# Low parts of the weights: which of them GpSimd makes and which VectorE, in a three-block transformer kernel

## The chip, the cores and the metric

The kernel runs on one core of one Trainium2 chip. The metric is the time of the device for one launch, in microseconds, median of three runs. The engines of the core are TensorE (PE in the profile, with its weight loads as PEld), VectorE (DVE), ScalarE (ACT), GpSimd (POOL) and SyncE (SP, which here only issues loads and stores).

## What is computed

256 tokens of width 1024 pass through a chain of residual parts, all in fp32:

```python
h = x
h = h + even_mixer(rmsnorm(h), ...)        # 1024 -> 2048, conv and pooling, -> 1024
h = h + conv_ffn(rmsnorm(h), ...)          # 1024 -> 2 x 2816, silu, -> 1024
h = h + odd_mixer(rmsnorm(h), ...)         # 16 heads of attention
h = h + conv_ffn(rmsnorm(h), ...)
h = rmsnorm(h)                             # end of the first block
h = h + attention_2(rmsnorm(h), ...)       # stick-breaking and differential heads
h = h + conv_ffn_2(rmsnorm(h), ...)        # gelu, both halves convolved
h = h + sigmoid(rmsnorm(h) @ w_ple_gate) * (p @ w_ple_proj)
return rmsnorm(h)
```

The products with weights are made in three passes. A weight w is rounded to its high part wh, the rest w - wh is its low part wl, the input is split in the same way, and TensorE adds wh·xh, wh·xl and wl·xh. So each weight tile costs one rounding (ScalarE), one subtraction (VectorE or GpSimd) and three matmuls.

## The kernel before, in words

**Tiling.** Channels lie on the 128 partitions, the 256 tokens along the free dimension. A *unit* is 128 output channels: 8 tiles of 128x128 weights (1024 columns), 11 in the down phases (1408 columns, half of the 22 input chunks), 10 in the last phase (1280 columns). Four units are a *quad*, and a ring of four slots `s` = 0 to 3 in `raw`, `wh` and `wl` holds one quad; as soon as TensorE is done with the unit in a slot, the unit one quad later can be made in its place.

**Phases** (`PHASES`, name and quads): even_in 4, even_out 2, up0 11, down0 4, qkv0 6, out0 2, up1 11, down1 4, qkv1 6, out1 2, up2 11, down2 4, ple 2. A phase works on its own results and at the same time makes the weights one quad ahead: in its last quad these are the weights of the first quad of the next phase (`ahead`). So the first quad of up1 is made in the last quad of out0, and so on. Three units of the second quad of out0 and out1 (`early_units`) are kept in free room of `ys` and are made already at the end of the attention.

**The steps of one unit.** SP loads `raw[s]` when the low part of the quad before is made (`lo_ready[s]`). ScalarE waits for the load and for TensorE to leave the slot, and rounds `wh` (line 480, `hi_ready`). Then `wl = raw - wh` is made by GpSimd (line 434) if the slot is in `POOL_SLOTS` of the phase, else by VectorE (line 785, called by `split_ahead`); both raise `lo_ready[s]`, on which TensorE waits (lines 1243 to 1245 are the three matmuls of a tile). In `POOL_SLOTS` slots 0 and 2 of every phase are GpSimd's, none in qkv0 and qkv1, all four in ple.

**The order** is written out by hand in each engine's program, one block for an engine, and semaphores join them; nothing is scheduled by a tool. What stands around the change:

- `residual_out` (even_out, out0, out1). For each of 8 chunks m of `h`: VectorE adds the result to `h` (line 928, `bank_read`), then makes a low part of the weights if the slot is its own, then the low part of the next layer's input `xs` (line 801), then adds the square into `acc` (line 809). ScalarE between them makes the high part of `xs` (line 502) and the square (497). The next phase's first two units wait on TensorE for the chunks of `xs` one after the other.
- `residual_down`: the same for two chunks in a quad (line 950 adds).
- `up`: per quad two pairs of gate and value; VectorE reads the bank (824), does the taps of the convolution (833), the product (975) and its low part (979), and its `split_ahead` stands before the read of the next bank.
- `attention`: at the end VectorE makes the low part of an output (828), for layer 1 scales `h` by the norm in the middle (line 1182), and goes on to `residual_out`, whose first step clears `acc` (918).
- ple: per chunk VectorE reads (824), `split_ahead`, adds the square of the chunk before (809), multiplies by the gate (1215) and adds to `h` (1218); ScalarE rounds the weights ahead (480), makes the sigmoid (768), waits for `h`, squares it (497) and scales it (774). After the last chunk come the statistics, the root, the last scaling and the stores.

Of the kernel before, what the change touches and what calls it, by code (L numbers as in the profile page):

```python
# [55 lines left out]
PHASES = [("even_in", 4, DC), ("even_out", 2, DC), ("up0", 11, DC), ("down0", 4, HALF),  # L56
          ("qkv0", 6, DC), ("out0", 2, DC), ("up1", 11, DC), ("down1", 4, HALF),
          ("qkv1", 6, DC), ("out1", 2, DC), ("up2", 11, DC), ("down2", 4, HALF),
          ("ple", 2, DC + PLE)]


POOL_SLOTS = {name: (0, 2) for name, _, _ in PHASES} | {"qkv0": (), "qkv1": (), "ple": (0, 1, 2, 3)}


VECTORS = [("mix0", DC), ("ffn0", DC), ("mix1", DC), ("ffn1", DC), ("attn2", DC), ("ffn2", DC),
# [10 lines left out]
def build_program(nc, streams, x_in, p_in, vectors_in, pool_in, gate_in, rel_in, onehot_in, count_in, out):  # L76
# [4 lines left out]
    base, total = {}, 0  # L81
# [28 lines left out]
    def ahead(name, i, s):  # L110

        if isinstance(i, int) and i == quads_of[name] - 1:
            return (follow[name][0], base[follow[name][0]]) if name in follow else (None, None)
        return name, i + (base[name] + 1)
# [6 lines left out]
    def is_early(name, i, s):  # L121

        return isinstance(i, int) and (base[name] + i + 1, s) in early_units

    def final_unit(name, i, s):

        return isinstance(i, int) and i == quads_of[name] - 1 and s == RING - 1
# [4 lines left out]
    with ExitStack() as ctx:  # L132
# [189 lines left out]
        def split_weights(q, s, width):  # L322

            if isinstance(q, int) and (q, s) in early_units:
                at = PAIRS * 2 * SEQ + s * 2 * DC * P
                return flat_ys[:, at:at + DC * P], flat_ys[:, at + DC * P:at + 2 * DC * P]
            return wh[:, s, 0:width], wl[:, s, 0:width]
# [94 lines left out]
        @block.gpsimd  # L422
        def _(pool):
            steps = Steps(pool, pool_step)

            def split_phase(name, first, end, slots=None):
                tiles = tiles_of[name]

                def split_quad(i):
                    q = i + base[name]  # L430
                    for s in slots or POOL_SLOTS[name]:
                        pool.wait_ge(hi_ready, q * RING + s + 1)
                        high, low = split_weights(q, s, tiles * P)
                        nc.gpsimd.tensor_tensor(low, raw[:, s, 0:tiles * P], high.bitcast(f32), ALU.subtract)\  # L434
                          .then_inc(lo_ready[s], 1)

                if name in ("out0", "out1"):
                    for i in range(first, end):
                        split_quad(i)
                else:  # L440
                    each_quad(pool, first, end, split_quad)

            def pick(out_ap, compare, fill, at, pattern, per_row):
                return nc.gpsimd.affine_select(out=out_ap, in_=out_ap, compare_op=compare, fill=fill, base=at, pattern=pattern,
                                               channel_multiplier=per_row)


            split_phase("even_in", 0, 1, slots=(2,))
            nc.gpsimd.memset(neg_ones[:, :], -1.0)
            nc.gpsimd.memset(not_past, 0.0)  # L450
            nc.gpsimd.memset(neg_tri[:, :], -1.0)
            nc.gpsimd.memset(ident[:, :], 0.0)
            steps(nc.gpsimd.memset(sel_raw, 0.0))
            split_phase("even_in", 1, 2)
            pick(ident[:, :], ALU.not_equal, 1.0, 0, [[-1, P]], 1)
            pick(neg_tri[:, :], ALU.is_ge, 0.0, 0, [[-1, P]], 1)
            pick(not_past, ALU.is_gt, NEG, 0, [[1, P]], -1)
            split_phase("even_in", 2, 3)
            steps(pick(sel_raw, ALU.not_equal, HD ** 0.5, 0, [[-1, HEADS], [0, P]], 1))
            split_phase("even_in", 3, 4)  # L460
            pick(sel_raw, ALU.not_equal, HD ** 0.5, -HD, [[-1, HEADS], [0, P]], 1).then_inc(masks_ready, 1)
            for name, quads, _ in PHASES[1:]:
                if POOL_SLOTS[name]:
                    split_phase(name, 0, quads)

            pool.wait_ge(gained, POOL_OUT)
            pool.wait_ge(last_scale, 1)
            for m in range(POOL_OUT):
                nc.gpsimd.tensor_tensor(h[:, m, :], h[:, m, :], rstd[:, :], ALU.mult).then_inc(pool_out_ready, 1)
# [308 lines left out]
        def _(dve):  # L778
            steps = Steps(dve, dve_step)

            def split_unit(q, s, tiles):

                dve.wait_ge(hi_ready, q * RING + s + 1)
                high, low = split_weights(q, s, tiles * P)
                nc.vector.tensor_tensor(low, raw[:, s, 0:tiles * P], high.bitcast(f32), ALU.subtract).then_inc(lo_ready[s], 1)  # L785

            def split_ahead(name, i, s):

                target, q = ahead(name, i, s)
                if target and s not in POOL_SLOTS[target]:  # L790
                    split_unit(q, s, tiles_of[target])

            def phase(name, body, per_quad=0):
# [412 lines left out]
            for i in range(quads_of["ple"]):  # L1206
                q = i + base["ple"]
# [458 lines left out]
```

## Time and profile before

| | before |
|---|---|
| median of three runs | 968.26 us (967.33 to 969.67) |
| the profiled execution | 968.35 us, its span 966.6 us |
| PE busy | 934.3 us, 97% |
| PEld busy | 910.7 us, 94% |
| DVE busy | 649.6 us, 67% |
| ACT busy | 526.6 us, 54% |
| POOL busy | 314.7 us, 33% |
| mean granted clock of TensorE | 0.987 of full speed |

The profile is of one execution. Its times are counted from the first instruction; 1.75 us of the 968.35 lie outside the span. A timeline row gives start, duration, engine, line, operation, and in brackets the idle time of the engine before it with what ended it. Two instructions of one engine can overlap by some 0.1 us, since the record of one ends after the next has begun.

### The profile page before, as it was taken

To read this page: it belongs to the slowest core of one execution; us is meant where nothing else is said; L and a number is where in the kernel's file an instruction comes from. 1 tells how busy PE (TensorE), PEld (TensorE's weight loads), DVE (VectorE), ACT (ScalarE), POOL (GpSimd) and SP (SyncE) were. 2 spreads that over 40 slices of the span, in tenths; PEclk is the share of its full clock that TensorE was granted. 3 is DMA by queue.
4 is the path that set the end of the run, shared out by engine and by line. 5 is a ranking of instruction groups with operands and counts; after the bars stand their busy time and mean duration, and the time that the engine had idled before them with its cause. 6 is when DMAs were issued, how large, how long until landed. Compare 5 with 4: busy or idle time off the path is not lost.

```text
span 966.6 us, 20895 instructions
## 1 busy us (share of the span) xinstructions
PE 934.3 (97%) x7618; PEld 910.7 (94%) x7618; DVE 649.6 (67%) x1133; ACT 526.6 (54%) x847; POOL 314.7 (33%) x134
## 2 busy tenths in 40 slices
PE   8899999999998999999999999999999999999993
PEld 7789999999997999999999999989999999999993
DVE  6998676665456776676666555797557877765376
ACT  6345665555444555575555544556557766654443
POOL 3343343444410001334443441000224434444552
PEclk9899999999999999999999999999999999999997
DMA  7535865567542533375556754344335655665421
GB/s 245 184 110 196 229 221 192 183 201 251 183 146 87 171 135 119 123 234 186 186 175 195 233 182 135 125 155 141 107 106 180 194 187 185 188 218 192 159 81 45
DMA packets 46329, 163.52 MB, mean 169 GB/s; under 512 B 5010, under 2 KB 9746, under 8 KB 46277
## 3 DMA queue, kind: packets, MB, share of 16 engines
q1 hardware_dynamic: 41704, 158.19, 49.6%
q10 hardware_dynamic: 4573, 4.62, 1.8%
q8 instruction: 34, 0.56, 0.2%
q14 instruction: 18, 0.15, 0.0%
HBM read 161.71 MB, written 3.44 MB: 171 GB/s over the span
## 4 chain that ended last, share of the span: by engine, by line
PE 80%; DVE 8%; issue 6%; ACT 3%; POOL 1%; DMA 1%; SPq 0%; DVEq 0%; POOLq 0%; ACTq 0%
PE psum L1243 25%; PE psum L1244 24%; PE psum L1245 24%; POOL wl L434 1%; DVE h L1218 1%; PE psum L1415 1%; DMA raw<-in_even_in 1%; DVE wl L785 1%; ACT wh L480 1%; DVE work L882 1%; PE psum L1392 1%; DVE xs L801 1%; PE psum L1384 1%; PE psum L1356 1%; ACT xs L502 0%
## 5 line engine op out<-in xcount | busy, mean ns | idle before, releaser
L434 POOL TENSOR_TENSOR wl<-raw,wh 128x1024 fp32r<-128x1024 f32 (+2 forms) x113 | 297.3, 2631 | 614.9 <-ACT wh L480 614.8
L1243 PE MATMUL psum<-xs,wh 128*128 128x256 f32 x1632 | 467.8, 287 | 6.9 <-DVE wl L785 4.2
L1244 PE MATMUL psum<-xs,wh 128*128 128x256 f32 x1632 | 462.9, 284 | 0.0
L1245 PE MATMUL psum<-xs,wl 128*128 128x256 f32 x1632 | 462.8, 284 | 0.0
L480 ACT ACTIVATE wh<-raw 128x1024 fp32r<-128x1024 f32 (+2 forms) x270 | 301.2, 1119 | 264.6 <-PE psum L1245 252.8
L1243 PEld LDWEIGHTS psum<-xs,wh 128*128 128x128 f32 x1632 | 314.4, 193 | 13.7 <-DVE wl L785 5.4
L1244 PEld LDWEIGHTS psum<-xs,wh 128*128 128x128 f32 x1632 | 314.4, 193 | 0.2
L1245 PEld LDWEIGHTS psum<-xs,wl 128*128 128x128 f32 x1632 | 314.3, 193 | 0.0
L785 DVE TENSOR_TENSOR wl<-raw,wh 128x1024 fp32r<-128x1024 f32 (+1 forms) x157 | 203.9, 1301 | 99.4 <-ACT wh L480 99.0
L1243 PE MATMUL psum<-ys,wh 128*128 128x256 f32 x672 | 191.8, 285 | 0.0
L1244 PE MATMUL psum<-ys,wh 128*128 128x256 f32 x672 | 190.7, 284 | 0.0
L1245 PE MATMUL psum<-ys,wl 128*128 128x256 f32 x672 | 190.7, 284 | 0.0
L1243 PEld LDWEIGHTS psum<-ys,wh 128*128 128x128 f32 x672 | 129.6, 193 | 0.8 <-issue 0.7
L1244 PEld LDWEIGHTS psum<-ys,wh 128*128 128x128 f32 x672 | 129.6, 193 | 0.1
L1245 PEld LDWEIGHTS psum<-ys,wl 128*128 128x128 f32 x672 | 129.5, 193 | 0.0
L833 DVE SCALAR_TENSOR_TENSOR psum<-work,vec,psum 128x256 f32<-128x256 f32 x176 | 85.3, 485 | 56.1 <-ACT psum L591 53.0
L801 DVE SCALAR_TENSOR_TENSOR xs<-h,vec,xs 128x256 fp32r<-128x256 f32 (+1 forms) x56 | 61.0, 1098 | 29.1 <-ACT xs L502 28.7
L824 DVE TENSOR_TENSOR work<-psum,rstd 128x256 f32<-128x256 f32 x112 | 47.1, 421 | 19.8 <-PE psum L1245 19.1
L591 ACT ACTIVATE psum<-work,vec 128x256 f32<-128x256 f32 x88 | 49.4, 561 | 9.7 <-DVE work L824 9.4
L502 ACT ACTIVATE xs<-h,vec 128x256 fp32r<-128x256 f32 (+1 forms) x48 | 24.3, 506 | 40.4 <-DVE h L928 26.5
L641 ACT ACTIVATE work<-work,row_max 128x128 f32<-128x128 f32 (+1 forms) x48 | 21.3, 444 | 34.5 <-DVE row_max L1045 25.8
L1019 DVE TENSOR_TENSOR qkv<-psum,rstd 128x256 f32<-128x256 f32 x48 | 19.7, 418 | 15.7 <-PE psum L1245 15.7
(195 smaller groups left out, 708.6 us busy)
## 6 DMA issues: line engine op xcount, KB each, us to landing
raw<-in_up SPq DMA_DIRECT2D x132, 512.0 KB, 3.8
raw<-in_down SPq DMA_DIRECT2D x48, 704.0 KB, 4.3
raw<-in_qkv SPq DMA_DIRECT2D x48, 512.0 KB, 3.3
raw<-in_even_in SPq DMA_DIRECT2D x16, 512.0 KB, 4.2
raw<-in_out SPq DMA_DIRECT2D x16, 512.0 KB, 3.2
raw<-in_ple SPq DMA_DIRECT2D x8, 640.0 KB, 3.9
raw<-in_even_out SPq DMA_DIRECT2D x8, 512.0 KB, 3.3
toeplitz_dram<-table_dram ACTq DMA_DIRECT2D x1, 2048.0 KB
```

Of the source, the lines that this page charges most:

```text
L434: nc.gpsimd.tensor_tensor(low, raw[:, s, 0:tiles * P], high.bitcast(f32), ALU.subtract)\
L480: nc.scalar.activation(split_weights(q, s, tiles * P)[0], raw[:, s, 0:tiles * P], ACT.Copy).then_inc(hi_ready, 1)
L502: nc.scalar.activation(xs[:, ds(m, 1), 0, :], h[:, ds(m, 1), :], ACT.Identity, scale=column(VECTORS[n][0], m)).then_inc(xh_ready, 1)
L591: nc.scalar.activation(target, padded[:, 2:2 + SEQ], ACT.Identity, bias=column(bias_name, chunk), scale=column(taps, chunk + 2 * chunks)). ...
L641: last = nc.scalar.activation(e[:, half, a:z], e[:, half, a:z], ACT.Exp, bias=row_max[:, n % 2, at:at + 1], accum_out=row_sum[:, n % 2, at ...
L785: nc.vector.tensor_tensor(low, raw[:, s, 0:tiles * P], high.bitcast(f32), ALU.subtract).then_inc(lo_ready[s], 1)
L801: nc.vector.scalar_tensor_tensor(xs[:, ds(m, 1), 1, :], h[:, ds(m, 1), :], column(VECTORS[n][0], m), xs[:, ds(m, 1), 0, :].bitcast(f32), A ...
L824: return nc.vector.tensor_tensor(out_ap, proj[:, s, 0:SEQ], rstd[:, :], ALU.mult)
L833: return nc.vector.scalar_tensor_tensor(out_ap, padded[:, k:k + SEQ], column(taps, chunk + k * chunks), out_ap, ALU.mult, ALU.add)
L1243: nc.tensor.matmul(bank, high_w[:, w], high, start=first, stop=False)
L1244: nc.tensor.matmul(bank, high_w[:, w], low, start=False, stop=False)
L1245: done = nc.tensor.matmul(bank, low_w[:, w], high, start=False, stop=last)
```

## The change

`POOL_SLOTS` now has two entries for each phase: the slots that GpSimd makes in the first quad of the phase, and those in the others. A new helper `pool_slots(name, q)` picks the entry. GpSimd keeps slots 0 and 2 in the up phases behind their first quad, in even_in (slot 2 alone in the first quad), and in the first quad of even_out, out0 and out1. Everything else is VectorE's: the first quads of the up phases, the second quads of even_out, out0 and out1, the down phases and ple.

```diff
-POOL_SLOTS = {name: (0, 2) for name, _, _ in PHASES} | {"qkv0": (), "qkv1": (), "ple": (0, 1, 2, 3)}
+POOL_SLOTS = {name: ((), ()) for name, _, _ in PHASES}
+POOL_SLOTS |= {"even_in": ((2,), (0, 2)), "even_out": ((0, 2), ()), "out0": ((0, 2), ()), "out1": ((0, 2), ())}
+POOL_SLOTS |= {name: ((), (0, 2)) for name in ("up0", "up1", "up2")}
...
+    def pool_slots(name, q):
+
+        return POOL_SLOTS[name][0 if isinstance(q, int) and q == base[name] else 1]
...
-            def split_phase(name, first, end, slots=None):
+            def split_phase(name, first, end):
...
-                    for s in slots or POOL_SLOTS[name]:
+                    for s in pool_slots(name, q):
...
-                if POOL_SLOTS[name]:
-                    split_phase(name, 0, quads)
+
+                first, others = POOL_SLOTS[name]
+                if first:
+                    split_phase(name, 0, 1)
+                if others:
+                    split_phase(name, 1, quads)
...
-                if target and s not in POOL_SLOTS[target]:
+                if target and s not in pool_slots(target, q):
```

Counted over the program, GpSimd makes 117 low parts before and 73 after; 44 go to VectorE: 2 in even_out, 2 in the first quad of each up phase, 8 in each down phase, 2 in each of out0 and out1, and 8 in ple. No instruction of TensorE, ScalarE or SP is moved. Lines of the changed program are numbered 12 higher on VectorE (785 is 797, 1218 is 1230).

VectorE in ple, from the reciprocal of the norm on. Before:

```order
L819 RECIPROCAL rstd<-work 128x256
L918 MEMSET acc 128x256
L824 TENSOR_TENSOR work<-psum,rstd 128x256
L1215 TENSOR_TENSOR work<-psum,work 128x256
L1218 TENSOR_TENSOR h<-h,work 128x256
L824 TENSOR_TENSOR work<-psum,rstd 128x256
L809 TENSOR_TENSOR acc<-acc,work 128x256
L1215 TENSOR_TENSOR work<-psum,work 128x256
L1218 TENSOR_TENSOR h<-h,work 128x256
```

And after:

```order
L831 RECIPROCAL rstd<-work 128x256
L930 MEMSET acc 128x256
L836 TENSOR_TENSOR work<-psum,rstd 128x256
L797 TENSOR_TENSOR wl<-raw,wh 128x1280
L1227 TENSOR_TENSOR work<-psum,work 128x256
L1230 TENSOR_TENSOR h<-h,work 128x256
L836 TENSOR_TENSOR work<-psum,rstd 128x256
L797 TENSOR_TENSOR wl<-raw,wh 128x1280
L821 TENSOR_TENSOR acc<-acc,work 128x256
L1227 TENSOR_TENSOR work<-psum,work 128x256
L1230 TENSOR_TENSOR h<-h,work 128x256
```

In each of the first four chunks a low part of 1280 columns now stands between the read of the bank and the square.

VectorE at the end of the second attention (layer 1), going over into the residual of out1; `ys<-raw,ys` is the low part of an early unit. Before:

```order
L1092 SCALAR_TENSOR_TENSOR work<-work 128x768
L785 TENSOR_TENSOR ys<-raw,ys 128x1024
L1182 SCALAR_TENSOR_TENSOR h<-h,vec,mid_rstd 128x256
L828 TENSOR_TENSOR ys<-psum,ys 128x256
L1182 SCALAR_TENSOR_TENSOR h<-h,vec,mid_rstd 128x256
L918 MEMSET acc 128x256
L928 TENSOR_TENSOR h<-h,psum 128x256
```

And after:

```order
L1104 SCALAR_TENSOR_TENSOR work<-work 128x768
L797 TENSOR_TENSOR ys<-raw,ys 128x1024 x2
L1194 SCALAR_TENSOR_TENSOR h<-h,vec,mid_rstd 128x256
L840 TENSOR_TENSOR ys<-psum,ys 128x256
L797 TENSOR_TENSOR ys<-raw,ys 128x1024
L1194 SCALAR_TENSOR_TENSOR h<-h,vec,mid_rstd 128x256
L930 MEMSET acc 128x256
L940 TENSOR_TENSOR h<-h,psum 128x256
```

Two early low parts are new on this engine; the second of them stands right ahead of the first addition into `h`.

VectorE in the last quad of the residual of out1 (chunks 4 to 6), where the first quad of up2 is made. Before:

```order
L928 TENSOR_TENSOR h<-h,psum 128x256
L801 SCALAR_TENSOR_TENSOR xs<-h,vec,xs 128x256
L809 TENSOR_TENSOR acc<-acc,psum 128x256
L928 TENSOR_TENSOR h<-h,psum 128x256
L785 TENSOR_TENSOR wl<-raw,wh 128x1024
L801 SCALAR_TENSOR_TENSOR xs<-h,vec,xs 128x256
L809 TENSOR_TENSOR acc<-acc,psum 128x256
```

And after:

```order
L940 TENSOR_TENSOR h<-h,psum 128x256
L797 TENSOR_TENSOR wl<-raw,wh 128x1024
L813 SCALAR_TENSOR_TENSOR xs<-h,vec,xs 128x256
L821 TENSOR_TENSOR acc<-acc,psum 128x256
L940 TENSOR_TENSOR h<-h,psum 128x256
L797 TENSOR_TENSOR wl<-raw,wh 128x1024
L813 SCALAR_TENSOR_TENSOR xs<-h,vec,xs 128x256
L821 TENSOR_TENSOR acc<-acc,psum 128x256
```

Chunk 4 (and chunk 6 like it) now has a low part of 1024 columns on VectorE between its addition and its `xs`, as chunk 5 had before.

## Rows read from the trace of the kernel before

**Rows 1.** Busy time by stretch: us, PE, PEld, DVE, ACT, POOL (instructions), granted clock, DMA share, GB/s.

```profile
40.00:47.00 7.00, 7.00 (x26) 4.80 (x25) 5.85 (x11) 0.89 (x2) 0.00 (x0) 0.51 0.50 173
...
140.00:290.00 150.00, 150.00 (x1252) 150.00 (x1252) 87.37 (x142) 76.29 (x109) 57.23 (x21) 1.00 0.58 192
...
313.00:316.40 3.40, 3.40 (x18) 2.78 (x15) 3.37 (x7) 1.22 (x3) 0.00 (x0) 0.50 0.60 173
```

**Rows 2.** Waits of PE: line waited for, us in total, times, longest.

```profile
PE psum L1517 <- DVE work L891: 4.8, 2, 2.6
...
PE psum L1243 <- DVE xs L801: 2.5, 2, 1.3
PE psum L1392 <- DVE work L1065: 2.4, 1, 2.4
PE psum L1559 <- POOL wl L434: 1.2, 1, 1.2
```

**Rows 3.** Groups with shapes apart: busy us, mean ns | idle before.

```profile
L785 DVE TENSOR_TENSOR wl<-raw,wh 128x1024 fp32r<-128x1024 f32 x133 | 162.8, 1227 | 51.2 <-ACT wh L480 50.8
...
L785 DVE TENSOR_TENSOR wl<-raw,wh 128x1408 fp32r<-128x1408 f32 x24 | 41.1, 1712 | 48.2 <-ACT wh L480 48.2
...
L434 POOL TENSOR_TENSOR wl<-raw,wh 128x1280 fp32r<-128x1280 f32 x8 | 23.6, 2955 | 18.2 <-ACT wh L480 18.2
```

**Rows 4.** Timeline of DVE in the last quad of out0, chunks 4 to 6.

```profile
407.48 0.41 DVE L928 TENSOR_TENSOR h<-h,psum 128x256 f32<-128x256 f32 x1
...
410.51 0.41 DVE L928 TENSOR_TENSOR h<-h,psum 128x256 f32<-128x256 f32 x1
...
411.98 0.47 DVE L801 SCALAR_TENSOR_TENSOR xs<-h,vec,xs 128x256 fp32r<-128x256 f32 x1
...
412.71 0.41 DVE L928 TENSOR_TENSOR h<-h,psum 128x256 f32<-128x256 f32 x1
413.76 1.69 DVE L801 SCALAR_TENSOR_TENSOR xs<-h,vec,xs 128x256 fp32r<-128x256 f32 x1 [0.65 <-ACT xs L502]
```

**Rows 5.** Timeline of POOL and PE in the same stretch.

```profile
412.80 2.38 POOL L434 TENSOR_TENSOR wl<-raw,wh 128x1024 fp32r<-128x1024 f32 x1 [2.82 <-ACT wh L480]
...
415.51 0.38 PE L1243 MATMUL psum<-xs,wh 128*128 128x256 f32 x1 [1.35 <-DVE xs L801]
```

**Rows 6.** Timeline at the entry of out1's residual, DVE and PE.

```profile
714.40 0.42 DVE L828 TENSOR_TENSOR ys<-psum,ys 128x256 fp32r<-128x256 f32 x1 [1.60 <-ACT ys L544]
714.75 1.06 DVE L1182 SCALAR_TENSOR_TENSOR h<-h,vec,mid_rstd 128x256 f32<-128x256 f32 x1
...
716.23 0.42 DVE L928 TENSOR_TENSOR h<-h,psum 128x256 f32<-128x256 f32 x1
...
716.84 0.32 PE L1243 MATMUL psum<-ys 128*128 128x256 f32 x1
```

**Rows 7.** Timeline of DVE in ple: chunks 2, 3 and 7.

```profile
939.68 2.52 DVE L1218 TENSOR_TENSOR h<-h,work 128x256 f32<-128x256 f32 x1
...
944.56 0.42 DVE L1215 TENSOR_TENSOR work<-psum,work 128x256 f32<-128x256 f32 x1 [1.45 <-ACT work L768]
945.02 2.48 DVE L1218 TENSOR_TENSOR h<-h,work 128x256 f32<-128x256 f32 x1
...
955.36 0.42 DVE L1218 TENSOR_TENSOR h<-h,work 128x256 f32<-128x256 f32 x1
```

**Rows 8.** Timeline of ACT and PE in ple.

```profile
942.96 1.25 ACT L480 ACTIVATE wh<-raw 128x1280 fp32r<-128x1280 f32 x1
...
947.27 0.39 PE L1559 MATMUL psum<-ps,wh 128*128 128x256 f32 x1 [1.21 <-POOL wl L434]
```

**Rows 9.** Timeline: PE in up0's second quad; ACT and DVE at up2's end.

```profile
107.85 0.38 PE L1243 MATMUL psum<-xs,wh 128*128 128x256 f32 x1 [0.18 <-POOL wl L434]
...
857.18 1.38 ACT L480 ACTIVATE wh<-raw 128x1408 fp32r<-128x1408 f32 x1 [0.30 <-PE psum L1245]
...
857.74 0.41 DVE L824 TENSOR_TENSOR work<-psum,rstd 128x256 f32<-128x256 f32 x1
```

More of the change, by code:

```diff
@@ L445, in pick @@
                                                channel_multiplier=per_row)
-            split_phase("even_in", 0, 1, slots=(2,))
+            split_phase("even_in", 0, 1)
             nc.gpsimd.memset(neg_ones[:, :], -1.0)
```

## The prediction, made before the changed kernel was run

> **What bounds the kernel now.** I read the busy times by stretch first. In 140 to 290 us, which is up0 and down0, PE is busy all 150 us with 1252 matmuls, one every 0.12 us, at full clock, and DVE is busy 87 us and POOL 57 [rows 1]. The other up and down phases look the same. There TensorE alone sets the time, and work that goes from POOL to DVE is free as long as DVE keeps up. So only the places where PE waits can change. The list of PE's waits has them [rows 2]: 4.8 us on the pooling in even_in and 2.4 us in the first attention, neither near a moved instruction; 2.5 us on the `xs` chunks at out0 into up1 and out1 into up2; 1.2 us on a GpSimd low part in ple. Behind ple's last matmul the rest of the chain is DVE's and ACT's, so what DVE loses in ple is lost at the end.
>
> What the reader is to see in the timelines is how DVE and POOL hinder each other. The last `xs` low part before PE's wait (L801) took 1.69 us, the one before it, without POOL at work, 0.47 [rows 4]. It began at 413.76, behind a POOL low part that ran from 412.80 to 415.18, and it ended at 415.45, 0.27 us behind that [rows 5]. In ple L1218, two inputs from SBUF like L801, took 2.52 and 2.48 us beside POOL and 0.42 without [rows 7]. So a DVE instruction with two SBUF inputs that comes while POOL works waits until POOL is done. L928, which reads one input from PSUM, stays at 0.41 [rows 4].
>
> **The change part by part.** The sum is made against the profiled execution, 968.35 us with a span of 966.6; the median of the runs is 968.26, 0.1 below, which I leave out.
>
> Price of a moved low part on DVE: 1.22 us for 1024 columns [rows 3]. For 1408 columns the mean is 1.71 us, which holds some that waited for POOL [rows 3]; by the slope of 1024 columns a free one is 1.6. For 1280 columns, a size DVE never had, the two give 1.22 + 256 x 1.02 ns = 1.48. On POOL the same work is 2.96 [rows 3]. The 44 moved ones add some 62 us to DVE's 650, and nothing to PE.
>
> *Part 1, ple: on the path.* Take the end of L1218 as the beat. Before, it ends at 942.20 and 947.50, a beat of 5.3 us [rows 7]. In the beat ACT squares and scales, starts the rounding 0.76 us in and ends it at 2.01 [rows 8]; POOL starts on it, the gate follows, and L1218 waits for POOL. After, DVE makes the low part from 2.05 to 3.53, then the square (L809, 0.33 from start to start: L801 and L809 together take 0.73 from 411.98 to 412.71 [rows 4], 0.40 of it L801), then L1215 and L1218, 0.46 apart [rows 7], and 0.42 for the last: 3.45 + 0.34 + 0.46 + 0.42 = 4.67. The sigmoid is done by then. That is 0.65 a beat, and from chunk 0 to chunk 3 there are three: 1.95 us. Chunk 0 itself gains more: its L1218 loses its wait for POOL as well, some 1.9 us, against 1.48 for the low part, of which the wait for the gate hides about half a us; and in down2's last quad the `xs` low parts no longer wait for POOL, by which the norm's root comes some 0.6 us earlier. I take 1.65, from 0.6 to 1.8. The last four chunks go on at 2.07 a beat, (955.78 - 947.50) / 4 [rows 7], and the tail behind them doesn't change. PE isn't in the way: its last unit loses its wait of 1.21 and starts at 946.1 [rows 8], and with 30 matmuls of 0.12 it ends at 949.7, while the last L1218 would end at 955.8 - 3.6 = 952.2. **-3.6 us**, between -2.55 and -3.75.
>
> *Part 2, out0 into up1.* A step from addition to addition is 3.03 us with a POOL low part beside it (407.48 to 410.51) and 2.20 with a DVE one in it (410.51 to 412.71), since the DVE one lies in the 0.65 us in which DVE waits for ACT anyway [rows 4]. Chunks 4 and 6 change kind. Then chunk 6 is added at 407.48 + 2 x 2.20 = 411.88, and its `xs` is ready 1.94 us later (410.51 to 412.45 is the model), at 413.82, 1.63 us before the old 415.45. PE lost 1.35 by the record, 1.5 counted in its beat of 0.12 (the record of the last matmul lasts on), at 415.51 [rows 5]. Gain 1.5, with only 0.1 us of margin, so 0.8 to 1.5. Chunk 7 follows 1.8 later and is wanted 2.9 later. The early low part that is new ahead of out0's first addition is covered by DVE's wait for PE there. **-1.5 us**.
>
> *Part 3, out1 into up2.* The same two steps, but DVE has no pause at the entry. L828 at 714.40 is followed now by a low part of 1.22, then L1182, which loses its wait for POOL (1.06 becomes 0.47), then the addition: it moves from 716.23 to 716.23 + 1.13 - 0.59 = 716.77 [rows 6]. PE's first matmul of the second quad waits for that addition and started at 716.84, 0.2 us behind its end [rows 6]; now it starts at 717.3. Behind it are queued out1's whole second quad and up2. That is +0.45. Chunk 6 is ready 1.63 - 0.54 = 1.09 us earlier than before; PE, 0.45 late already, wants it 1.3 - 0.45 = 0.85 earlier: the wait, 2.5 - 1.35 = 1.15 by the record and 1.3 in PE's beat, is gone [rows 2, 5]. Bounds: +0.5 (the wait stays, too) to -1.3. **-0.85 us**.
>
> *Part 4, even_out into up0.* 0.18 us by the record, 0.3 in PE's beat, is lost at 107.85 on POOL's low part for up0's second quad [rows 9]. POOL still makes it, but the residual of even_out ends some 2 us earlier by the same steps, and ACT gets to that rounding earlier. **-0.3 us**, 0 to -0.3.
>
> *Part 5, down phases and the ends of the up phases: nothing.* A down quad lasts PE 132 x 0.12 = 15.8 us. DVE now has four low parts of 1.6 and two chunks of about 1.3 in it, 9 us; cover is 6 us, beyond which each us costs one, as it would in every quad. Its waits for ScalarE's rounding stand ahead of `xs`, which matters only in the last quad of down2, counted in part 1; down0 and down1 hand over to qkv, which VectorE made before, too. At the end of up2 two low parts of 1.6 come ahead of the read of the last bank, at 857.74 [rows 9]. PE had left the last unit of up2 by 857.18 and wants the bank 33 x 0.12 = 4.0 us later, at 861.1 [rows 9]. With the idle time that DVE had before its low parts I get the read's end at 860.0: 1.1 us of cover. up0 and up1, with fewer taps, have more.
>
> Sum: -3.6 - 1.5 - 0.85 - 0.3 = -6.25, so 968.35 - 6.25 = **962.1 us**. All parts at their bad ends give -2.55 - 0.8 + 0.5 = -2.85, 965.5; I set the end at 965.4, since not all four will fall there.
>
> *The clock.* After PE's waits of 2.6 and 2.4 us the granted clock went to 0.5, that is 1.2 GHz of 2.4, at 40 and at 313 us, for some 7 and 3.4 us [rows 1, 2]. Of the waits of up to 1.35 us none had such a stretch. In my forecast no new wait is over 0.5 us. A stretch of 3.4 us costs 1.7; the one at 313 us lies behind moved work and can go or double, which is +-1.7.
>
> The Trainium skill, TensorE: Matmul & The Clock Gate, Part 1, says that the window in which activity is judged runs freely, so that the same kernel can meet it at another phase. The two stretches of different length behind nearly equal waits agree with that. By it a shift alone could give 960.4 or 963.8 where the sum says 962.1.
>
> **Rivals.**
> - *Only ple gains.* The margin of part 2 is 0.1 us and part 3 has a loss of its own; if chunk 6 comes late in both, or waits turn up elsewhere, parts 2 to 4 are nothing: 968.35 - 3.6 = 964.7. For it: thin margins. Against: the 2.20 step is measured, not derived.
> - *A wash.* A POOL low part of 1024 columns holds up DVE for 1.2 us (1.69 less 0.47) and DVE's own takes 1.22 [rows 3, 4]: if the steps took as long with it, out0, out1 and ple would stay as they are, 968.3. Against: the step of 2.20, in which it hides behind ACT. In ple it can hide less, and there its 1.48 stands against 2.1 of waiting. The Trainium skill, Perfetto Trace Analysis, Optimizing Scalar/DVE Operations, says that the two engines share a read port, so that offloading between them might not help; read the other way round, it says that bringing work back might change nothing. The trace agrees on the sharing, and its steps of 3.03 and 2.20 speak against the second half. By that rule the time would be 968.3.
> - *Slower: DVE becomes the bound at the end of the up phases.* Without use of its idle time the two low parts put the last bank's read at 857.74 + 0.41 + 3.2 = 861.35, 0.25 us too late [rows 9]. The mechanism decides from 1.1 us more DVE work than I count; to make the kernel slower by 2 us it must eat the 6.25 as well, some 2.8 us at each of three places: 970.4. For it: this is where a moved low part stands ahead of a bank that PE needs. Against: nothing in the trace makes a DVE low part that slow but POOL, which is then silent.
> - *The change doesn't do what it says.* The order of instructions shows 44 moved; left out.
>
> **How the numbers follow.** The forecast, 960.4 to 964.4 with the clock's share, has 0.78; only ple, 964.7 (964.4 to 965.4), 0.10; the wash 0.07; slower 0.04; 0.01 is left for more gain than that. The range reaches from 960.0 to 965.4 and holds nearly 0.85. A measurement of this kernel can tell 0.2%, some 2 us, from no change; the cases give 0.88 faster, 0.08 within, 0.04 slower.
>
> **What would show it.** POOL busy falls from 315 to some 195 us, DVE's busy time rises by less than 62 us, since its waits behind POOL count as busy. L1218 is 0.42 in all eight chunks and the beat 4.7. PE's waits on L801 and on POOL in ple are gone; a new one of 0.4 to 0.5 us stands at the first matmul of out1's second quad. The low parts of 1408 columns on DVE have a mean of 1.6. I am wrong if PE waits in the down phases or at the banks of the last up quads, if the step of chunks 4 and 6 stays near 3.0, or if a new stretch at half clock follows one of these places.

## The result, and the profile after

The changed kernel takes 957.78 us (median of four runs, 956.27 to 959.12), the kernel before, in the same comparison, 967.83 (967.33 to 969.67): a ratio of 0.9903, 95% interval 0.9886 to 0.992. The forecast was 962.1, from 960.0 to 965.4. So the direction was right and the size was not: it is faster by 10 us here, and by some 8 us in the later comparisons (0.9916 and 0.9923). The forecast had 6.25. One run of the kernel before in a later comparison, 1002.13 us at a granted clock of 0.843, is a slow one and is left out of every mean below.

The profiled execution takes 957.83 us, with a span of 955.6. Busy times, after:

```profile
PE 930.6 (97%) x7618; PEld 908.9 (95%) x7618; DVE 663.7 (69%) x1177; ACT 525.6 (55%) x847; POOL 184.3 (19%) x90
```

GpSimd lost 130 us of work, and VectorE, which took it over, gained 14, where the forecast had put its new low parts at some 62. The groups with shapes apart (busy us, mean ns | idle before) say why; they answer [rows 3]:

```profile
L442 POOL TENSOR_TENSOR wl<-raw,wh 128x1024 fp32r<-128x1024 f32 x73 | 176.5, 2418 | 656.9 <-ACT wh L492 656.8
L797 DVE TENSOR_TENSOR wl<-raw,wh 128x1024 fp32r<-128x1024 f32 x141 | 172.9, 1229 | 53.7 <-ACT wh L492 53.5
L797 DVE TENSOR_TENSOR wl<-raw,wh 128x1408 fp32r<-128x1408 f32 x48 | 77.9, 1623 | 44.5 <-ACT wh L492 44.4
L813 DVE SCALAR_TENSOR_TENSOR xs<-h,vec,xs 128x256 fp32r<-128x256 f32 x38 | 17.8, 480 | 8.2 <-ACT xs L514 7.8 <-ACT xs L538 0.4
L797 DVE TENSOR_TENSOR wl<-raw,wh 128x1280 fp32r<-128x1280 f32 x8 | 11.9, 1493 | 10.5 <-ACT wh L492 10.5
```

The prices were right: 1408 columns take 1.62 us now (1.71 before, with waits behind GpSimd in it; forecast 1.6), 1280 take 1.49 (forecast 1.48). The `xs` low part, which had taken up to 2.93 us (a mean of 1.10), is 0.47 to 0.49 everywhere. What VectorE's record called busy had in part been waiting.

The waits of PE (line waited for, us in total, times, longest) answer [rows 2]:

```profile
PE psum L1529 <- DVE work L903: 4.8, 2, 2.6
...
PE psum L1404 <- DVE work L1077: 2.4, 1, 2.4
...
PE psum L1255 <- DVE h L940: 0.3, 1, 0.3
```

The waits on the `xs` chunks and the two on GpSimd's low parts are gone, and the new one at out1 is there. The waits left out of the list stand at the same places as before: at the start and in the mixer on VectorE's first low parts, in the attentions, and at the last statistics (2.2 us now, 4.4 before). Nothing has taken their place in the down phases.

**out0 into up1**, VectorE's timeline of chunks 5 to 7 after, answering [rows 4]:

```profile
404.65 0.41 DVE L940 TENSOR_TENSOR h<-h,psum 128x256 f32<-128x256 f32 x1
...
406.84 0.41 DVE L940 TENSOR_TENSOR h<-h,psum 128x256 f32<-128x256 f32 x1
407.17 1.21 DVE L797 TENSOR_TENSOR wl<-raw,wh 128x1024 fp32r<-128x1024 f32 x1
408.31 0.47 DVE L813 SCALAR_TENSOR_TENSOR xs<-h,vec,xs 128x256 fp32r<-128x256 f32 x1
...
409.04 0.41 DVE L940 TENSOR_TENSOR h<-h,psum 128x256 f32<-128x256 f32 x1
```

Every step (from addition to addition) is 2.20 us, where a step beside GpSimd had been 3.03.

**out1**, first step, DVE and PE, answering [rows 6]:

```profile
708.19 1.22 DVE L797 TENSOR_TENSOR ys<-raw,ys 128x1024 fp32r<-128x1024 f32 x1
709.32 0.48 DVE L1194 SCALAR_TENSOR_TENSOR h<-h,vec,mid_rstd 128x256 f32<-128x256 f32 x1
...
710.22 0.42 DVE L940 TENSOR_TENSOR h<-h,psum 128x256 f32<-128x256 f32 x1
...
710.79 0.35 PE L1255 MATMUL psum<-ys 128*128 128x256 f32 x1 [0.35 <-DVE h L940]
```

**ple**, DVE from chunk 1's addition to chunk 2's, and PE's first matmul behind the last chunk, answering [rows 7, 8]:

```profile
926.73 0.43 DVE L1230 TENSOR_TENSOR h<-h,work 128x256 f32<-128x256 f32 x1
...
929.20 1.49 DVE L797 TENSOR_TENSOR wl<-raw,wh 128x1280 fp32r<-128x1280 f32 x1 [1.71 <-ACT wh L492]
...
931.40 0.42 DVE L1230 TENSOR_TENSOR h<-h,work 128x256 f32<-128x256 f32 x1
...
944.48 0.74 PE L1581 MATMUL psum<-acc,ones 128*128 128x256 f32 x2 [2.22 <-DVE work L1227]
```

The beat is 4.67 us (926.73 to 931.40), as worked out, and the multiply-and-add into `h` is 0.42.

**The end of up2**, answering [rows 9]: the last bank's read stands at

```profile
852.15 0.42 DVE L836 TENSOR_TENSOR work<-psum,rstd 128x256 f32<-128x256 f32 x1
```

All of up2 lies 7.41 us earlier than before (the statistics matmul ahead of it, explained in the next section: 735.54 before, 728.13 after). Without the two low parts ahead of it the read would stand at 857.74 - 7.41 = 850.33, so they moved it by 1.82 us; the forecast had its end go from 858.15 to 860.0, 1.85. PE doesn't wait for it.

### The profile page after: what moved, and what is told of

The parts are those of the page before. It is cut to its first block, busy times and chain, and to the rows that moved or that the text cites. A ratio compares the mean times of both kernels' runs of the same rounds, so it can differ in the third digit from the quotient of the medians.

```text
span 955.6 us, 20828 instructions
## 1 busy us (share of the span) xinstructions
PE 930.6 (97%) x7618; PEld 908.9 (95%) x7618; DVE 663.7 (69%) x1177; ACT 525.6 (55%) x847; POOL 184.3 (19%) x90
## 4 chain that ended last, share of the span: by engine, by line
PE 88%; DVE 8%; ACT 2%; issue 1%; DMA 1%; SPq 0%; DVEq 0%; ACTq 0%
PE psum L1255 28%; PE psum L1256 27%; PE psum L1257 27%; DVE work L894 2%; DVE wl L797 1%; PE psum L1427 1%; DMA raw<-in_even_in 1%; PE psum L1404 1%; PE psum L1396 1%; ACT wh L492 1%; PE psum L1368 0%; PE psum L1366 0%; ACT work L653 0%; DVE work L836 0%; DVE acc L865 0%
## 5 line engine op out<-in xcount | busy, mean ns | idle before, releaser
L797 DVE TENSOR_TENSOR wl<-raw,wh 128x1024 fp32r<-128x1024 f32 (+2 forms) x197 | 262.8, 1336 | 108.8 <-ACT wh L492 108.4
L442 POOL TENSOR_TENSOR wl<-raw,wh 128x1024 fp32r<-128x1024 f32 x73 | 176.5, 2418 | 656.9 <-ACT wh L492 656.8
L813 DVE SCALAR_TENSOR_TENSOR xs<-h,vec,xs 128x256 fp32r<-128x256 f32 (+1 forms) x56 | 26.5, 480 | 8.2 <-ACT xs L514 7.8
```

Source lines behind the costliest of these rows:

```text
L813: nc.vector.scalar_tensor_tensor(xs[:, ds(m, 1), 1, :], h[:, ds(m, 1), :], column(VECTORS[n][0], m), xs[:, ds(m, 1), 0, :].bitcast(f32), A ...
```

## Where the time went, stretch by stretch

The sums of squares of the norms are made by a statistics matmul, which stands at a fixed place in PE's order; from one to the next PE has the same work in all kernels of this study. Four of their rows, before (a second execution of it) and after (a third):

```profile
290.84 0.60 PE L1274 MATMUL psum<-acc,ones 128*128 128x256 f32 x2
417.58 0.60 PE L1274 MATMUL psum<-acc,ones 128*128 128x256 f32 x2
```

```profile
288.98 0.60 PE L1286 MATMUL psum<-acc,ones 128*128 128x256 f32 x2
412.83 0.60 PE L1286 MATMUL psum<-acc,ones 128*128 128x256 f32 x2
```

Differences of such starts, us (each column one profiled execution; the variants are those of the experiments below):

| stretch | before | before, 2nd | after | after, 3rd | ple alone | up1's quad back |
|---|---|---|---|---|---|---|
| start to first statistics | 19.38 | 18.38 | 18.42 | 18.26 | 18.14 | 18.63 |
| to up0 (even mixer) | 81.95 | 81.18 | 79.65 | 79.83 | 81.17 | 81.11 |
| to qkv0 (up0, down0) | 191.12 | 191.28 | 190.71 | 190.89 | 190.50 | 190.50 |
| to up1 (attention, out0) | 126.74 | 126.74 | 123.86 | 123.85 | 125.28 | 125.28 |
| to qkv1 (up1, down1) | 190.50 | 190.50 | 190.49 | 190.50 | 190.50 | 190.50 |
| to up2 (attention, out1) | 125.85 | 125.87 | 125.00 | 125.02 | 125.87 | 124.99 |
| to ple (up2, down2) | 188.34 | 188.34 | 188.35 | 188.33 | 188.34 | 188.34 |
| to the last statistics | 31.60 | 31.58 | 28.00 | 27.99 | 28.00 | 27.99 |

The four places gave, between the recorded executions before and after, 3.60 in ple, 0.85 at out1, 0.41 in up0, and at out0 a part of 2.88. The rest of the 11.0 us of span is elsewhere: 0.96 at the start, where the first weights landed later in the first execution (its first weight matmul stood at 9.95 us, and at 8.1 to 9.3 in the others here), 2.30 in the even mixer, and the other part of the 2.88.

The 2.88 are 1.43 for the wait at out0 (put back in experiment 3) and 1.46 for a stretch at half clock that the first execution after doesn't have (priced in the section on the clock). Of the 2.30, one stretch of 3.4 us less is some 1.5. Most of the rest is a wait of 0.64 us on a low part of the weights that stands in this one trace alone:

```profile
28.13 0.39 PE L1243 MATMUL psum<-xs,wh 128*128 128x256 f32 x1 [0.64 <-DVE wl L785]
```

The second execution of the kernel before has the same stretches at half clock, not this wait, and 81.18 us there.

## The experiments

**1. The same two kernels again.**

> The kernel before, unchanged, to have its start and its stretches at half clock a second time. The places that the change touches account for 6.3 us of the 10; the other 4 lie ahead of or beside it: the first matmul on weights began 1.1 us earlier in the changed kernel's trace, 0.6 us more was gained by 28 us, and the trace has two stretches of half clock less (3 us). Theory A (chance of the execution): here the first matmul on weights starts anywhere from 8.8 to 10.0 us and the stretches at half clock differ in number or length from the first trace, while the waits behind moved work (1.35, 1.15 and 1.21 us) come back to within 0.1 us; ratio 1.000 to the kernel before, with single runs spread over 3 us. Theory B (something in the changed program brings it): start at 9.95 and stretches at 40, 70 and 313 us come back as they were.

> The changed kernel, unchanged. Theory A: over more runs the gain shrinks towards the 6.3 us of the named places, ratio 0.9925 to 0.9935, and single runs differ by 1.7 us steps with the mean granted clock (one stretch of 3.4 us each). Theory B: the gain stays at 10 us, ratio 0.989 to 0.991, start at 8.9 us.

> The kernel before once more, for its granted clock. Theory A1 (the short waits of 1.2 to 1.5 us at out0, out1 and in ple can be followed by half clock, depending on the execution): a stretch at half clock near 412, 730 or 945 us in one of the executions. A2 (only the long ones of 2.2 us and more): stretches only near 40, 70 and 310 us, as in both traces so far.

The kernel before again: 966.14 us (ratio 0.9987, 0.9973 to 1.0001); one more execution of it 967.84. The changed one: 958.32, ratio 0.9916, 0.9896 to 0.9936. All waits were there again with the same size (1.36, 1.16 and 1.19 us before; 0.35 after). So the waits belong to the kernels. The late start does not.

**2. One part alone.** Against the changed kernel's table, all phases as before but ple:

```diff
-POOL_SLOTS = {name: ((), ()) for name, _, _ in PHASES}
-POOL_SLOTS |= {"even_in": ((2,), (0, 2)), "even_out": ((0, 2), ()), "out0": ((0, 2), ()), "out1": ((0, 2), ())}
-POOL_SLOTS |= {name: ((), (0, 2)) for name in ("up0", "up1", "up2")}
+POOL_SLOTS = {name: ((0, 2), (0, 2)) for name, _, _ in PHASES}
+POOL_SLOTS |= {"even_in": ((2,), (0, 2)), "qkv0": ((), ()), "qkv1": ((), ()), "ple": ((0, 1, 2, 3), (0, 1, 2, 3))}
+POOL_SLOTS |= {"ple": ((), ())}
```

> Only ple's low parts go to VectorE, all else as before. From the places: -3.6 us, ratio 0.9963, L1218's twin at 0.42 in all chunks. Theory A: 0.9963 within 0.001. Theory B, if the extra comes with any change of the program's instructions: 0.992 to 0.993.

Measured: 962.56, ratio 0.9961 (0.9946 to 0.9976). In its trace the last stretch of the table is 28.00 against 31.6. Four of the others are those of before (81.17, 190.50 in up1, 125.87 and 188.34), and the waits at out0 and out1 are there; two are shorter without any moved work: 190.50 in up0, where PE has no wait on GpSimd's low part this time, and 125.28 at the attention, which here has no stretch at half clock:

```profile
309.00:313.00 4.00, 3.92 (x33) 3.42 (x34) 4.00 (x6) 2.58 (x4) 0.00 (x0) 1.00 0.32 93
```

Part 1 is worth 3.60 us and nothing of it depends on the other parts.

The same, with ple all GpSimd's as before, and the out phases and the up phases' first quads changed:

```diff
+POOL_SLOTS |= {name: ((0, 2), ()) for name in ("even_out", "out0", "out1")}
+POOL_SLOTS |= {name: ((), (0, 2)) for name in ("up0", "up1", "up2")}
```

> Only the second quads of even_out, out0, out1 and the first quads of the up phases go to VectorE. From the places: -0.3 -1.5 -0.85 = -2.65 us, ratio 0.9973; PE's waits on the xs chunks gone, one of 0.35 at out1's second quad. Theory A: 0.9973 within 0.001. Theory B: 0.993.

> The change at even_out, out0, out1 and the first quads of the up phases alone. Theory: apart from the clock it gives 2.9 us (its counted 2.65 and little more), and the rest that it showed before (5.4 in all) is fewer half-clock stretches; its mean number of them lies between that of the kernel before and that of the changed kernel, if that number has something to do with the short waits, or at either, if it is chance. Rival: the ratio goes to 0.997, so the first timing was chance.

Measured: 962.01, ratio 0.9944 (0.9925 to 0.9964), and 961.46, ratio 0.995 (0.9934 to 0.9966). Counted from the profile it should have been 0.9973, which lies outside both intervals. In both traces the `xs` waits are gone, the 0.35 at out1 is there and ple waits as before, so the places do what was forecast, and some 2 us more come from somewhere else. The clock is about half of that: by the table in the next section these runs have 2.9 us less at half clock than those of before, some 1.2 us of time. The other 1 us stays open.

And the down phases alone:

```diff
+POOL_SLOTS |= {name: ((), ()) for name in ("down0", "down1", "down2")}
```

> Only the 24 low parts of the down phases go to VectorE. Theory A (what is left over beside the 6.3 us of the places is TensorE's clock, by where the waits fall): ratio 0.999 to 1.001, PE without a wait in the down phases, VectorE's low part of 1408 columns at 1.6 us. Theory B (the down phases bring the rest, 2 us): 0.998 or less, and a wait of PE in the kernel before that is gone here.

Measured: 966.19, ratio 0.9998 (0.9984 to 1.0011). 24 of the 44 moved low parts bring nothing, as part 5 said.

**3. The wait at out0, put back.** In the changed kernel:

```diff
-POOL_SLOTS |= {name: ((), (0, 2)) for name in ("up0", "up1", "up2")}
+POOL_SLOTS |= {name: ((), (0, 2)) for name in ("up0", "up2")}
+POOL_SLOTS |= {"up1": ((0, 2), (0, 2))}
```

> The changed kernel, but the first quad of up1, made in the last quad of out0, has slots 0 and 2 back on GpSimd. Theory (part 2 of the forecast): this alone brings back the wait of 1.35 us on the xs chunk at the entry of up1, and costs 1.5 us, so 1.5 us above the changed kernel of the same call (+-0.5 for the clock); the waits at up2 and ple stay gone. Rival (the waits at out0 and out1 are what now and then brings a stretch at half clock): the wait is back and the run's mean clock falls as well, by 1.7 us or more on average, so 3 us or more above the changed kernel.

> The changed kernel, unchanged. Theory: 8 to 9 us below the kernel before, of which 6 us are the four places and the rest fewer stretches at half clock, whose number differs from run to run; with those taken off each run, 6.1 us below. Rival (the ple, out0 and out1 places give more than the 6.25 us counted): 8 us or more below with the half-clock time taken off too.

Its timeline, DVE, POOL and PE:

```profile
409.01 0.41 DVE L941 TENSOR_TENSOR h<-h,psum 128x256 f32<-128x256 f32 x1
410.06 1.70 DVE L814 SCALAR_TENSOR_TENSOR xs<-h,vec,xs 128x256 fp32r<-128x256 f32 x1 [0.65 <-ACT xs L515]
...
412.02 0.41 DVE L941 TENSOR_TENSOR h<-h,psum 128x256 f32<-128x256 f32 x1
```

```profile
409.11 2.38 POOL L443 TENSOR_TENSOR wl<-raw,wh 128x1024 fp32r<-128x1024 f32 x1 [2.83 <-ACT wh L493]
...
411.82 0.39 PE L1256 MATMUL psum<-xs,wh 128*128 128x256 f32 x1 [1.18 <-DVE xs L814]
```

The step beside GpSimd is 3.01 again, the low part of `xs` 1.70, the wait 1.18, and the stretch to up1 125.28 against 123.85: **1.43 us** for part 2, forecast 1.5. The times of the runs don't show it: 959.04 us against 958.79, ratios 0.9919 (0.9905 to 0.9933) and 0.9923 (0.9907 to 0.9938). The means are 959.1 and 959.0, and the runs of each spread over some 2.6 us. Two things stand against the 1.43. The changed kernel's runs have 0.5 us more outside the span (2.25 against 1.78), so the mean spans differ by 0.6 us (957.3 and 956.8). And the runs with the wait were less at half clock, which is worth some 0.9 us when the tail is taken off as in the section on the clock. The wait is back and the mean clock of its runs did not fall, it rose (0.992 against 0.990). So the rival, that the short waits at out0 bring stretches at half clock, falls.

**4. More of the same change.** In the changed kernel, VectorE makes all low parts of even_in behind its first quad:

```diff
+POOL_SLOTS |= {"even_in": ((2,), ())}
```

> The changed kernel, and also the low parts that even_in makes ahead from its quad 1 on go to VectorE; GpSimd keeps slot 2 of the very first quad. The pooling steps (two SBUF inputs) took 1.65 us in the mean beside GpSimd and 0.43 would be free. Theory A: the waits of PE on the pooling (2.6 and 2.2 us) shrink to 0.5 to 1.5, and with them the half-clock stretches at 40 and 70 us go: 3 to 6 us faster than the changed kernel, ratio to the kernel before 0.985 to 0.988. Rival C: VectorE's own 1.22 us takes the place of the wait: same as the changed kernel, 0.991.

Measured: 953.11, ratio 0.9866 (0.983 to 0.9902). The pooling steps were held up by GpSimd, too; their line, in the changed kernel and here:

```profile
L894 DVE TENSOR_TENSOR work<-work 128x256 f32<-128x256 f32 x10 | 15.8, 1582 | 0.3
```

```profile
L895 DVE TENSOR_TENSOR work<-work 128x256 f32<-128x256 f32 x10 | 6.2, 621 | 0.3
```

So the waits on the pooling, which the forecast had put aside as not near a moved instruction, were of the same kind as those that it counted. PE's waits on the pooling (2.6 and 2.2 us) are gone, short ones on low parts and on the mixer's output (1.55 and 0.86) have come, and at 40 and 70 us the clock stays full:

```profile
38.00:42.00 4.00, 4.00 (x32) 3.79 (x32) 3.82 (x9) 1.16 (x4) 0.00 (x0) 1.00 0.81 256
```

With even_out's first quad VectorE's too:

```diff
-POOL_SLOTS |= {"even_in": ((2,), (0, 2)), "even_out": ((0, 2), ()), "out0": ((0, 2), ()), "out1": ((0, 2), ())}
+POOL_SLOTS |= {"even_in": ((2,), (0, 2)), "out0": ((0, 2), ()), "out1": ((0, 2), ())}
...
+POOL_SLOTS |= {"even_in": ((2,), ())}
```

> The changed kernel with VectorE making all low parts of even_in behind its first quad and the first quad of even_out too, so GpSimd works in even_in's slot 2 once, in the first quads of out0 and out1 and in the up phases. Theory: the second pooling wait stays away as in the variant of even_in alone, and the entry of even_out has no short wait on GpSimd or VectorE that costs over 0.3 us: 953 +-1 us, the same as that variant. Rival (VectorE is late at the entry of even_out, where the pooling fills it): a wait of 1 to 2 us there and 955 us.

Measured: **951.96 us** (951.12 to 954.51), ratio 0.9857 (0.9837 to 0.9877), the lowest time of this study, though the four runs each of this kernel and of the one above overlap. The stretch to up0 is 72.28 us, 7.4 under the changed kernel's, and the wait of 0.86 is gone as well; besides the 4.8 us of waits it holds what the half-clock stretches behind them cost.

**5. Where it stops.** No GpSimd low part but the first:

```diff
-POOL_SLOTS |= {"even_in": ((2,), (0, 2)), "even_out": ((0, 2), ()), "out0": ((0, 2), ()), "out1": ((0, 2), ())}
-POOL_SLOTS |= {name: ((), (0, 2)) for name in ("up0", "up1", "up2")}
+POOL_SLOTS |= {"even_in": ((2,), ())}
```

> All low parts but one of the very first quad go to VectorE, also those of the up phases. VectorE is busy some 75 of 120 us in up2 and would get 20 more of 1.22, that is 100 of 120. Theory A (TensorE bounds the up phases): the same as with even_in alone moved, within 1 us. Rival D (VectorE becomes the bound in up2, where a value chunk costs two taps more, or its low parts come too late): PE waits in up2, 5 to 20 us slower than with even_in alone moved.

Measured: 963.13, ratio 0.997 (0.9955 to 0.9986): nearly all is given back. The mixer gains (72.36 us to up0), up0 and up1 lose only 0.6 and 0.3, but up2 and down2 take 199.12 us where all others take 188.34. In up2 both halves are convolved; VectorE is busy 52.9 of 60 us there, and PE waits. The stretch 750 to 810 us, in the columns of [rows 1]:

```profile
750.00:810.00 60.00, 58.49 (x469) 56.51 (x468) 52.90 (x99) 36.62 (x58) 0.00 (x0) 1.00 0.52 167
```

The same stretch in the changed kernel:

```profile
750.00:810.00 60.00, 60.00 (x502) 60.00 (x501) 46.27 (x97) 38.48 (x64) 26.45 (x11) 1.00 0.55 186
```

and two of PE's waits, the first repeated every 12.32 us (a quad takes 11.5 in the changed kernel), the other once at the end of up2:

```profile
838.43 0.38 PE L1254 MATMUL psum<-xs,wh 128*128 128x256 f32 x1 [0.26 <-DVE wl L796]
...
857.52 0.36 PE L1254 MATMUL psum<-ys,wh 128*128 128x256 f32 x1 [2.36 <-DVE work L835]
```

In each quad PE loses 0.8 us in its beat, at this wait and at a shorter hold half a quad later, both on VectorE's low parts: some 8 of the 10.8 us. The wait of 2.36 us, which is on the read of the last bank, is most of the rest. That is the place that the "slower" rival named, but the greater part of the loss is at the low parts in every quad, which it didn't name. VectorE was late at 88% busy, with idle time left. In the stretch above 6.4 us of it stand at the convolution's steps, which wait for ScalarE's step (L602), as here:

```profile
774.35 0.49 DVE L844 SCALAR_TENSOR_TENSOR psum<-work,vec,psum 128x256 f32<-128x256 f32 x1 [0.72 <-ACT psum L602]
```

The order of VectorE's work is fixed, so nothing else can fill that time. This is read from the trace; no variant with another order was run.

## The clock: what the forecast had too small

Three places of the kernel before have a stretch at half clock (1.2 GHz), each behind a wait of PE of over 2 us: two poolings and the attention. Its second execution, in the columns of [rows 1]:

```profile
38.60:45.40 6.80, 6.80 (x26) 5.12 (x26) 5.53 (x11) 0.89 (x2) 0.00 (x0) 0.50 0.48 178
69.30:72.70 3.40, 3.40 (x18) 3.40 (x17) 3.22 (x7) 0.48 (x1) 0.00 (x0) 0.50 0.37 131
311.70:315.10 3.40, 3.40 (x17) 3.29 (x16) 3.37 (x6) 0.89 (x2) 0.00 (x0) 0.50 0.73 184
```

The first execution after:

```profile
40.00:43.80 3.80, 3.80 (x21) 3.80 (x21) 3.62 (x8) 0.42 (x1) 0.00 (x0) 0.55 0.74 278
67.70:71.20 3.50, 3.50 (x18) 3.42 (x17) 3.33 (x7) 0.47 (x1) 0.00 (x0) 0.51 0.36 125
308.00:312.00 4.00, 3.95 (x33) 3.45 (x34) 4.00 (x6) 2.55 (x4) 0.00 (x0) 1.00 0.32 114
```

In the first line the clock is low from 40.4 us on. One stretch of 6.8 has become one of 3.4, and the one behind the attention's wait is missing, though PE waited the same 2.4 us. The table prices it: with a stretch there and the wait at out0 it is 126.74 to up1, with the wait alone 125.28, with neither 123.85. So **a stretch of 3.4 us costs 1.46 us** there (1.52 by the two traces of the out phases alone, 125.17 with it and 123.65 without). In the 14 traces of this study none stands anywhere but behind these three waits and in the tail, where PE has nothing to do. A long wait is not enough to bring one: the attention's wait of 2.4 us was followed by a stretch in 7 of the 14 traces, and the wait of 2.30 us on the first weights (at 9.95 us, before) and that of 2.36 at up2's end in the kernel without GpSimd by none. They vary from one execution to the next with nothing changed: behind the first pooling, which lies ahead of every moved instruction, the changed kernel had 3.4, 3.4 and 6.8 us in its three traces.

What a run lost can be read from its granted clock: time at half clock is 2 x span x (1 - clock). Means over the runs of a kernel, worked out so (for the first four runs of the kernel before no clock is on record, so they aren't in it):

| kernel | runs | us | at half clock, us |
|---|---|---|---|
| before | 66 | 966.6 | 24.0 |
| down phases alone | 10 | 966.4 | 23.9 |
| ple alone | 10 | 962.8 | 19.8 |
| out phases alone | 11 | 961.7 | 21.1 |
| changed | 16 | 958.5 | 18.5 |
| changed, up1's quad back | 6 | 959.1 | 15.3 |
| even_in VectorE's | 4 | 953.3 | 13.8 |
| even_in and even_out VectorE's | 4 | 952.4 | 15.7 |
| no GpSimd | 10 | 963.0 | 12.3 |

Of it the tail is 12.0 us before and 10.5 after (means of three traces each). It costs next to nothing: from the last statistics matmul to the end it is 11.13 to 11.16 us in 13 of the 14 traces, with 9.5 to 13.0 us of tail. The rest is 12.0 and 8.0 us: 4.0 us less at half clock, at 1.46 for 3.4 some 1.7 us.

The mean times differ by 8.1 us, but the mean spans by 8.6 (964.9 and 956.2). Outside the span lie 1.74 us in the runs of before and 2.25 in those of the changed kernel (2.15 with even_in VectorE's, 1.7 to 1.8 in all other variants); no run here tells why. Of the 8.6 the clock takes 1.7, and 6.9 are left. The places were counted at 6.25 and measured at 5.9, and up to 0.9 more in up0. So the account closes to within the 1 us that these shares are good for, and not better.

The Trainium skill, TensorE: Matmul & The Clock Gate, Part 1, says that the window in which activity is judged runs freely. The traces agree, as far as equal waits were followed by 3.4, 6.8 or no us at half clock. What stays open is why the changed kernel has fewer on average. Ple alone, whose moved work all lies behind the last of the three waits, seems to have had fewer, too (19.8, of it 9.5 tail in its one trace, so 10.3 in the body against 12.0); but the tails of two executions of one kernel, the out phases alone, were 13.0 and 10.5, so this is hardly clear of chance. The kernel with the wait at out0 put back had the fewest of those that keep the poolings' waits. So nothing here ties the number to the waits that the change removes. Whether it is a phase that goes with the length of the program or with the moment of its launch, no run here tells. The clock of a run is given to 0.001, that is 1.9 us at half clock, so none of these shares is good to better than some 1 us.

## Why the forecast was wrong, step by step

- *Part 1, ple, -3.6*: 3.60. Beat 4.67, as worked out; three beats give 1.95 and chunk 0 1.65, as counted.
- *Part 2, out0, -1.5*: 1.43, by putting it back. The steps of 2.20 held in all chunks, and the thin margin of 0.1 us with them. The two traces of the out phases alone, set against those with the wait, give 1.57 and 1.63.
- *Part 3, out1, -0.85*: 0.85 and 0.86, the new wait of 0.35 (forecast 0.45 in PE's beat) among it.
- *Part 4, up0, -0.3*: 0.4 in both pairs of the table. With even_out's residual as before the stretch was 190.50 to 191.49 in five traces (190.50 in ple alone), with it changed 190.50 to 190.89 in six. The wait on that low part, 0.15 to 0.73 us where there was one, comes and goes from one execution to the next. The sign is as forecast, the size is not settled.
- *Part 5, nothing*: the down phases alone 0.9998 (0.9984 to 1.0011), the bank's read at up2's end 1.8 us later and covered.
- *The clock, +-1.7*: **this is the step that failed**. The text named stretches at 40 and at 313 us, let one of 3.4 us go or come, and priced it at 1.7. The trace had a third, at 70 us, and 13.7 us in all, which at the measured 1.46 each 3.4 us cost some 5.8; each could be longer, shorter or missing. Between the two profiled executions two stretches of 3.4 us went, 2.9 of the 4.3 us that the forecast missed.
- *The base*: the profiled execution of the kernel before had its first weights 1.0 us late and the wait of 0.64 us at 28 us, which its second execution didn't have, with the same stretches at half clock. The forecast had no term for that. Against it stand 0.5 us more outside the span. So 968.35 - 6.25 - 2.9 - 1.6 + 0.5 = 958.1, and the profiled execution measured 957.8.
- *How much of it was chance*: the first comparison had dear runs before and cheap ones after. 968.3 stands against a mean of 966.6 over 66 runs, 957.8 against 958.5 over 16, and over all runs the clock's share is 1.7 us, not 2.9. Taken from 966.6 the places alone give 960.3, in the range, but the changed kernel's mean of 958.5 lies outside it as well. A clock term that let every stretch of the trace go would have reached down by 5.8 us instead of 1.7, to 956.3, and held the result; the forecast gave 0.01 to more gain than its range.
- *A slip in the working*: the 44 low parts add, by the forecast's own prices, 12 x 1.22 + 24 x 1.6 + 8 x 1.48 = 64.9 us, not 62. No term of the sum rests on it.
- *The rivals*: only ple gains fell with the 1.43 us at out0 and the 0.85 at out1, and a wash with these and the 3.60 in ple. The slower one has a mechanism that exists, but not at this change: it takes the 20 other low parts of up2 (the kernel without GpSimd) until it bites, and then mostly at the low parts.

## What to carry over

Work out what a wait is worth from the beat of the step that it sits in, not from the length of the wait; done so, the three places that could be measured came out within 0.1 us of the count. But before a forecast of a few us, list every stretch at the low clock, price each, and treat all of them as free to go or come: one execution is a sample, of the clock and of the start, and a median of three can sit 1.7 us off. Work that two engines share is given out by phase: taking it from GpSimd paid where PE waited on work that GpSimd held up, brought nothing in the down phases, and gave 10.8 us away in up2, where VectorE came to 88% busy.

## What the runs showed of the hardware that was not expected

- Taking 130 us of work off GpSimd added only 14 us to VectorE's busy time: 44 low parts of 1.2 to 1.6 us, less the time in which instructions with two SBUF inputs had stood behind GpSimd's and counted as busy (L801's mean before was 1.10 us, 0.48 after, over 56 of them; L1218's 1.44 and 0.43, over 8). The Trainium skill, Perfetto Trace Analysis, Optimizing Scalar/DVE Operations, says of the shared port that offloading between the two might not help; in this kernel bringing work back did, 3.6 us in ple alone.
- Two inputs from SBUF are not the only form that GpSimd held up. The mixer's TENSOR_SCALAR, with one tensor input (and one value per partition), took 0.35 us three times in the changed kernel and 2.58 once, beside a low part that ran on GpSimd from 51.44 to 53.82:

```profile
51.40 2.58 DVE L912 TENSOR_SCALAR work<-work,vec 128x256 f32<-128x256 f32 x1
```

- Putting a wait of 1.43 us back, seen in the trace to the hundredth, moved the mean of six runs by 0.1: the clock's part and the time outside the span differed by about as much the other way. A comparison of medians can't see it, the stretch between two fixed matmuls can; away from waits such a stretch repeats within 0.02 us over 190.5 (up1 and down1, in 13 of the 14 traces).
